# A hybrid decoder layer on one core: the first tile's shifted rows are read one stage earlier

## The reference

```
h = rmsnorm(x, g_pre)
s5_x, s5_z, rw_p, rw_z, pl_x, pl_z, gate_cols = split(h @ w_in)        # 57 blocks of 128 columns
y_s5 = s5_mix(s5_x, ...)        # complex diagonal state-space scan
y_rw = rwkv_mix(rw_p, ...)      # RWKV-7 time mixing, state of 8 heads x 64 x 64
y_pl = pool_mix(pl_x, ...)      # trailing-window means over 2, 4, 8, 16 tokens
merged = sum over the branches of sigmoid(gate) * ((y * silu(z)) @ w_up)
x + rmsnorm(merged @ w_o, g_post)
```

```
prev = concatenate([shift_prev[:, None], pf[:, :-1]], axis=1)
pm = pf + (prev - pf) * mu
r, k, v, lw, la = split(pm)     # 512 + 512 + 512 + 64 + 64 = 1664 = 13 * 128 columns
```

## Time and profile before

| | before |
|---|---|
| three executions, median | 1402.5 us |
| the profiled execution's own time | 1399.56 us |
| its span, first to last instruction | 1397.8 us |
| TensorE matmul busy | 1322.9 us (95%) |
| VectorE / ScalarE / GpSimd busy | 760.2 / 449.5 / 397.3 us |
| mean granted TensorE clock | 0.979 of full speed |

### The profile page before, as it was taken

One profiled execution on the slowest core, in us unless ns is written; L12 is line 12 of the kernel. 1 busy time (PEld: TensorE's weight loads), 2 busy tenths in 40 slices (PEclk: granted clock), 3 DMA queues, 4 the chain that ended last, 5 costly groups with the idle time before them and its releaser, 6 DMA issues.

```text
span 1397.8 us, 32218 instructions
## 1 busy us (share of the span) xinstructions
PE 1322.9 (95%) x14024; PEld 1208.2 (86%) x14024; DVE 760.2 (54%) x1499; ACT 449.5 (32%) x809; POOL 397.3 (28%) x403
## 2 busy tenths in 40 slices
PE   5999999997999999999999999999999989899997
PEld 5898999987888988989898989988897589798885
DVE  7595744625444637173554637274453648989322
ACT  7222222221423425252432525252334521023211
POOL 7226656462031302222031212212111032254000
PEclk8999999999999999999999999999997999999999
DMA  8242433334512213122221313122116286455221
GB/s 231 84 110 77 121 86 95 87 101 116 157 60 66 83 44 96 59 73 66 78 72 45 94 60 95 59 55 67 53 56 221 49 258 196 133 180 177 97 85 38
DMA packets 167725, 139.07 MB, mean 99 GB/s; under 512 B 34143, under 2 KB 156688, under 8 KB 167456
## 3 DMA queue, kind: packets, MB, share of 16 engines
q1 hardware_dynamic: 157314, 119.69, 28.9%
q10 hardware_dynamic: 10270, 17.32, 4.1%
HBM read 91.36 MB, written 42.34 MB: 96 GB/s over the span
## 4 chain that ended last, share of the span: by engine, by line
PE 54%; DVE 9%; ACT 6%; issue 3%; DMA 1%; ACTq 1%; POOL 0%; SPq 0%; DVEq 0%
PE f_ps L363 11%; PE f_ps L365 9%; PE f_ps L364 9%; PE q L2245 9%; PE q L365 2%; PE q L364 2%; PE q L363 2%; DVE early L1971 2%; PE f_ps L2135 2%; PE q L2276 2%; ACT L1383 1%; DVE up_gu L1969 1%; PE q L2262 1%; DVE w_z L1797 1%; DMA f_out<-projected 1%
## 5 line engine op out<-in xcount | busy, mean ns | idle before, releaser
L363 PE MATMUL f_ps<-h_hi,fw_hi 128*128 128x384 f32 (+1 forms) x968 | 340.6, 352 | 14.1 <-ACTq L1371 5.6
L365 PE MATMUL f_ps<-h_hi,fw_lo 128*128 128x384 f32 (+1 forms) x968 | 317.3, 328 | 0.0
L1311 POOL TENSOR_TENSOR fw_lo<-fw,fw_hi 128x1024 fp32r<-128x1024 f32 x46 | 110.2, 2395 | 651.0 <-ACT fw_hi L1369 651.0
L364 PE MATMUL f_ps<-h_lo,fw_hi 128*128 128x384 f32 (+1 forms) x864 | 282.3, 327 | 0.0
L363 PEld LDWEIGHTS f_ps<-h_hi,fw_hi 128*128 128x128 f32 x968 | 182.6, 189 | 31.3 <-issue 10.0
L365 PEld LDWEIGHTS f_ps<-h_hi,fw_lo 128*128 128x128 f32 x968 | 182.9, 189 | 0.0
L364 PEld LDWEIGHTS f_ps<-h_lo,fw_hi 128*128 128x128 f32 x864 | 163.1, 189 | 3.9 <-issue 3.8
L1383 ACT ACTIVATE f_out<-f_ps 128x384 f32<-128x384 f32 (+1 forms) x108 | 51.1, 474 | 248.9 <-PE f_ps L365 248.4
L1787 DVE TENSOR_TENSOR t_m<-t_m,q 128x256 f32<-128x256 f32 (+1 forms) x66 | 27.6, 418 | 174.2 <-PE q L2245 174.2
L363 PE MATMUL proj_ps<-h_hi,fw_hi 128*128 128x384 f32 (+1 forms) x336 | 114.5, 341 | 4.8 <-ACT proj_out L943 3.7
L364 PE MATMUL proj_ps<-h_lo,fw_hi 128*128 128x384 f32 (+1 forms) x336 | 111.2, 331 | 0.0
(11 more groups left out here) (443 smaller groups left out, 2893.8 us busy)
## 6 DMA issues: line engine op xcount, KB each, us to landing
fw<-in_w_in_dram SPq DMA_DIRECT2D x50, 512.0 KB, 4.4
projected<-f_out SPq DMA_DIRECT2D x72, 192.0 KB, 2.0
f_out<-projected SPq DMA_DIRECT2D x48, 192.0 KB, 2.5
projected<-proj_out SPq DMA_DIRECT2D x16, 544.5 KB, 3.4
raw<-projected SPq DMA_DIRECT2D x8, 838.5 KB, 6.5
projected<-f_out SPq DMA_DIRECT2D x36, 160.0 KB, 1.8
branch_z<-projected ACTq DMA_DIRECT2D x8, 544.0 KB, 5.8
xt<-in_x_prompt_dram SPq DMA_DIRECT2D x8, 512.0 KB, 5.6
```

Of the source, the lines that this page charges most:

```text
L363: pe.matmul(out, whi, xhi, start=first, stop=False)
L364: pe.matmul(out, whi, xlo, start=False, stop=False)
L365: return pe.matmul(out, wlo, xhi, start=False, stop=last)
L1311: pool.tensor_tensor(wlo[:, g % 2], wst[:, g % 2], whi[:, g % 2].bitcast(F32), ALU.subtract).then_inc(fw_lo, 1)
```

## The change

The first tile's rows get a second name, `raw_first`, of 13 x 129 elements per partition, on the memory of `s5_ebuf` and `rot_tmp`. SP issues their load in the projection stage: behind the eight stores of the last S5 batch, ahead of `store_last`. Before it SP waits until the stores of the RWKV blocks have landed, until the last S5 table has been copied out of that memory, and until the rotations are made. Behind `store_last` SP waits for the rows too, so the stage's end holds that they have landed. In the RWKV stage `load_raw(0)` is gone, and the shift of tile 0 reads `raw_first` without a wait. Later tiles use `raw` as before, with the semaphore's counts moved down by one load.

```diff
         dtab, toep = sb("s5_dtab", [P, GB, L + 1, GC]), sb("s5_toep", [P, GB, P])
+        with nc.sbuf_tensor("raw_first", [P, RB, P + 1], F32) as e.raw_first:
+            pass
         ebuf_flat = sb("s5_ebuf", [P, GB * L * GC])
...
+        first_rows = sem("p_first_rows")
...
                         store_y((n - 10) // 4)
+                for r in range(R):
+                    sp.wait_ge(stored[r], 16 * len([n for n in range(WB + RB) if n % R == r]))
+                sp.wait_ge(toep_loaded, 16 * L * WB)
+                sp.wait_ge(rot_made, WB)
+                sp.dma_start(e.raw_first[:, :, :], e.scratch[B_RW:B_RW + RB, :, 0:P + 1].rearrange("b p t -> p b t")).then_inc(first_rows, 16)
                 store_last()
+                sp.wait_ge(first_rows, 16)
...
                 n = len(FILL_BLOCKS)
-                load_raw(0)
                 load_w(2)
...
-                    pm, cur = pms[i % 2][:, :, 0:T], raw[:, :, 1:P + 1] if t.prompt else raw[:, :, 0:T]
+                    rows = raw if i else e.raw_first
+                    pm, cur = pms[i % 2][:, :, 0:T], rows[:, :, 1:P + 1] if t.prompt else rows[:, :, 0:T]
                     if part == 0:
-                        dve.wait_ge(ev["raw_loaded"], i * 16 + 16)
+                        if i:
+                            dve.wait_ge(ev["raw_loaded"], i * 16)
                         if t.prompt:
-                            tt(pm, raw[:, :, 0:P], cur, ALU.subtract).then_inc(ev["shift"], 2)
+                            tt(pm, rows[:, :, 0:P], cur, ALU.subtract).then_inc(ev["shift"], 2)
```

## The result

The changed kernel takes 1405.18 us in the median of 20 executions, the kernel before 1401.34 us in the median of 20 beside it. The ratio is 1.0024 with a 95% interval of 1.0013 to 1.0035: slower by 3.4 us (1.8 to 4.9 us). The forecast was 3.3 us more. Its time of 1405.8 us stood on the median of three executions, 1402.5 us, which 20 executions put 1.2 us lower. The profiled execution took 1404.92 us, its span is 1403.2 us.

What follows compares the result with a forecast made beforehand. TensorE, busy 95% of the span, was taken as the bound, with SP's stores setting the RWKV stage's start. Terms 3.3 + 0 + 0 + 0 = 3.3 us on the 1402.5 median gave 1405.8 us, range 1403.3 to 1408.6.

Steps and rivals of the forecast that it cites:

- What sets the stage's start: Stage boundary: SP's stores alone set the RWKV stage's start while TensorE idles, so any added SP wait counts in full.
- The size: Load ahead of the last stores and barrier: costs 3.3 us, between 2.4 and 4.8 us.
- The way by latency: Load's landing before the barrier: 6.5 us after issue at 346.5, so 353.0, 3.4 us behind the former 349.57.
- the way by bytes: Queue before the barrier: 2.7 us for bytes at 315 GB/s, 0.3 slow start, 0.3 later store issue; sum 3.3 us.
- The shift: VectorE at the RWKV stage's head: `pm` ready 6 us after the start instead of 12.4, worth 0.
- The weights without the load beside them: RWKV stage's start: weight load issued 0.76 us earlier after the barrier, first used long after landing, worth nothing.
- The clock: TensorE behind the boundary restart: same 3.5 us at half clock, worth 0; bounds 0.5 us gain to 1.5 us cost.
- The hidden load: Rival at the boundary: load lands while SP still waits for its stores, 0 to +0.5 us; chance 0.07.
- the head bound by the rows: Rival in the RWKV stage's head: tile 0's chain sets its end, -3.2 us, 1399.3; chance 0.04.
- The change did what it says: Opposite rival: VectorE's wait would remain, about +3.3 us too; included in the forecast's 0.74.
- The clock's rival: Rival behind the boundary restart: slow stretch 2.9 us longer, 1.5 us of time, +4.8 us in all, 1407.3; chance 0.10.

Runs made afterwards that it cites:

- cross_ahead: Changed kernel with the load still ahead of the last stores, but waited for by VectorE behind the barrier instead of SyncE before it; ratio to kernel before 1.0038.
- early: Changed kernel with the load issued ahead of the last S5 batch's eight stores; ratio to the kernel before 0.9998.
- late: Kernel before with the load of tile 0's rows issued behind two weight loads of the RWKV stage; ratio 1.0005.
- head_early: Run early with tile 0's chain moved forward: low-rank products after 8 quarters, norms after 16, tanh behind the first chunk; ratio to the kernel before 0.9955.
- counts_only: Run early with only the counts moved: low-rank products after 8 quarters, norms after 16; ratio to the kernel before 0.9979.
- cross_behind: Changed kernel with the load behind the two last stores and waited for by VectorE in the RWKV stage; ratio to the kernel before 1.0007.
- behind: Changed kernel with the load issued behind the two last stores, still waited for before the barrier; ratio to the kernel before 1.0020.
- split: Changed kernel with 6 of 13 blocks loaded ahead of the last stores, the other 7 in the RWKV stage; ratio to the kernel before 1.0018.
- head_before: Kernel before with tile 0's chain moved forward as in head_early, load left in the RWKV stage; ratio 0.9983.
- tanh_only: Run early with only ScalarE's tanh for tile 0 moved behind the first chunk; ratio to the kernel before 0.9994.

## Why the prediction was right

**What sets the stage's start.** Said: SyncE's stores and nothing else, so that a landing added there counts in full. Shown: the pause of TensorE follows the last landing that SyncE waits for in every run (5.6 to 6.2 us where that landing was a store not held up by the load, 7.9 with 6 blocks, 9.5 to 9.7 with 13).

**The size.** Said: 3.3 us, with the load landing at 353.0 and the pause at 8.9 us. Measured: a pause 3.94 us longer in the profile, 3.4 us by the ratio. The mechanism was right, the split of the sum was not quite. The load itself was faster than forecast (5.5 us, where the shortest of the eight had been 6.5), and the stores behind it were last, by 1.5 us; the two misses have opposite signs. The way by latency had the wrong transfer last. In the way by bytes the terms that were too small are the 2.7 us for the bytes with 0.3 for the slow start (148 and 218 GB/s were moved for 3.5 us, not 315), and the 0.3 us for the later issue of the stores: counted from the last matmul, the second was issued 1.0 us later than before. That 3.3 meets the 3.4 of the ratio to a tenth is luck, with an interval from 1.8 to 4.9; the pause says 3.9. The rule of the Trainium skill that the prediction weighed, in "DMA: Bandwidth & Descriptors", section "Queues, rings and completion order", spoke of just this: increments land behind the earlier writes of the same DMA engine. Cross_ahead agrees with it: without SyncE's wait for the load the stores still took 6.0 us and landed behind it. The runs do not tell this rule from the stores' own bytes simply standing behind those of the load.

**The shift.** Said: `pm` 6 us into the stage, worth 0, its gain turning up in the wait for the gates. Shown: 11.9 against 5.0 us there, and in early a ratio of 0.9998. The cover is ScalarE's order, and its slack was measured in late: 3.6 us of delay, 0.9 us on TensorE's wait. What the prediction passed over is the 2.3 us wait ahead of the first turned features. It was there before the change, and head_early shows that it, with the 1.7 us, could be had.

**The weights without the load beside them.** Said: 0. Nothing in the profiles speaks against it; no run has it alone.

**The clock.** Said: 3.5 us at half clock behind the restart, unchanged, with a bound of 1.5 us. In the changed kernel it came back 3.8 us behind the restart. The bound was not idle: in counts_only it took 6.0. One reading was a little off: the 0.53 of 348.00 to 348.50 puts the fall at 348.0, not 348.3, and the 0.65 of 354.50 to 355.00 puts the return at 354.85, so the whole slow stretch was 6.8 us and not 6.4, and the bound 1.6 us.

**The rivals.** The hidden load is excluded by the pause of 9.5 us, the head bound by the rows by early. The change did what it says: VectorE no longer waits for the load. The clock's rival did not occur in the profile of the changed kernel; how often it does in others is open.

## What to carry to other kernels

A transfer that must land before a barrier costs as much as it moves the last landing if the other engines are already idle there (3.9 us here), and one queued ahead of the last stores delays them even if nobody waits for it; put it where the issuing engine has a gap long enough for the whole landing. A long wait on an engine off the critical path is no gain waiting to be had: look at what follows it in the order of the engines that consume it. Data that come earlier are worth something only when the order of work is changed to use them, and the two edits belong together (0.9998 and 0.9983 alone, 0.9955 together; the waits show it more surely than the times).

## What the runs showed of the hardware

A short wait on TensorE can cost more than its length. In most profiles a stretch of 3 to 3.5 us at half clock began within 1.7 us of the end of one of the two waits of tile 0's chain. In the kernel before, the changed one, early, cross_ahead and cross_behind it followed the 2.3 us wait. In behind and split it followed the 1.7 us wait and the 2.3 us wait had none; in late both waits had one; in head_before it followed the only one. In tanh_only the 2.3 us wait was followed by none, nor was the 0.8 us wait in counts_only. In head_early, without either wait, there was none. So neither wait brings the stretch for certain, and the first turned features are not its only place. Run behind at its 1.7 us wait (granted clock in the third column from the end):

```profile
371.50:374.50 3.00, 3.00 (x11) 3.00 (x10) 0.94 (x1) 2.03 (x8) 0.79 (x1) 0.51 0.20 44
```

After the pause at the boundary the half clock lasted 2.9 to 4.0 us from the first matmul in ten of the twelve profiles, 4.8 us in tanh_only and 6.1 us in counts_only.
